# A two-block model on one core: order of the latent projections, packing of the output weights, place of the turned-weight copy, and 16-bit one-hot rows

## What is computed

```python
experts = jnp.take_along_axis(cand_i, pos, axis=-1).reshape(PEER_BLOCK, PEER_HEADS * PEER_TOPK)
gates = jax.nn.softmax(top_s, axis=-1).reshape(PEER_BLOCK, PEER_HEADS * PEER_TOPK)
hid = jax.nn.gelu(jnp.einsum('nkd,nd->nk', u, xb), approximate=False) * gates
return jnp.einsum('nk,nkd->nd', hid, v_table[experts])
```

```python
h = xn @ w_in
q_lat, kv_lat, k_rope, z = jnp.split(h, [384, 640, 704], axis=-1)
q = (rms_norm(q_lat, q_norm) @ w_q_up).reshape(B, S, 16, 192)
kv = (rms_norm(kv_lat, kv_norm) @ w_kv_up).reshape(B, S, 16, 256)
# rotary part of q and k, causal softmax over 16 heads of width 128 -> o
return (o.reshape(B, S, 2048) * jax.nn.silu(z)) @ w_out
```

## Time and profile before

| | us |
|---|---|
| median of 3 runs | 3790.28 |
| lowest and highest | 3776.75, 3790.76 |
| the profiled execution, its own time | 3789.53 |
| its span in the trace | 3787.7 |
| mean granted clock of TensorE | 0.961 |
| TensorE busy in the span | 3565.3 |

### The profile page before, as it was taken

How to read it: one execution, slowest core, us unless ns; L and a number is a source line. 1 busy time by engine, 2 the same in 40 slices (tenths; PEclk the granted TensorE clock), 3 DMA queues, 4 the chain that set the end, 5 groups by cost and what they waited for, 6 DMA issues and landing times.

```text
span 3787.7 us, 45651 instructions
## 1 busy us (share of the span) xinstructions
PE 3565.3 (94%) x16352; PEld 2906.0 (77%) x16352; DVE 1827.5 (48%) x3647; ACT 1178.8 (31%) x1578; POOL 915.3 (24%) x371
## 2 busy tenths in 40 slices
PE   7999799999999998999999899989999989988998
PEld 6776578878888887888888688878887756666886
DVE  1354526974444535454554656454442343314573
ACT  3232334333444441121121332233332334423322
POOL 2301234442333334444454200000000421121000
PEclk8987899999999999999999899999999999989999
DMA  2200123444446455544545222222222211112222
GB/s 95 73 17 34 39 83 117 145 139 161 160 160 205 158 177 200 211 177 192 207 177 197 92 99 95 94 83 96 98 94 97 78 63 38 40 45 84 94 89 89
DMA packets 141175, 434.90 MB, mean 115 GB/s; under 512 B 11152, under 2 KB 44176, under 8 KB 132496
## 3 DMA queue, kind: packets, MB, share of 16 engines
q1 hardware_dynamic: 141072, 433.50, 32.8%
HBM read 364.25 MB, written 69.21 MB: 114 GB/s over the span
## 4 chain that ended last, share of the span: by engine, by line
PE 86%; issue 6%; DVE 3%; ACT 1%; DMA 1%; POOL 1%; SPq 0%; POOLq 0%; DVEq 0%; ACTq 0%
PE ring_banks L235 22%; PE ring_banks L237 22%; PE ring_banks L236 22%; PE work_banks L1064 3%; PE work_banks L237 3%; PE work_banks L235 3%; PE work_banks L236 3%; POOL wlo L709 1%; PE ring_banks L1225 1%; PE ring_banks L945 1%; PE work_banks L1194 1%; PE work_banks L1197 1%; PE work_banks L908 1%; DMA slot<-u 1%; PE work_banks L758 0%
## 5 line engine op out<-in xcount | busy, mean ns | idle before, releaser
L235 PE MATMUL ring_banks<-xx,wlo 128*128 128x512 f32 x2960 | 1178.1, 398 | 57.2 <-DVE xx L1674 39.7
L237 PE MATMUL ring_banks<-xx,whi 128*128 128x512 f32 x2960 | 1164.9, 394 | 0.0
L709 POOL TENSOR_TENSOR wlo<-slot,whi 128x1024 fp32r<-128x1024 f32 x235 | 578.9, 2467 | 2103.5 <-ACT whi L1277 2103.5
L236 PE MATMUL ring_banks<-xx,whi 128*128 128x512 f32 x2512 | 988.6, 394 | 0.0
L1277 ACT ACTIVATE whi<-slot 128x1024 fp32r<-128x1024 f32 x427 | 451.3, 1060 | 1073.9 <-DMA slot<-w 653.6
L235 PEld LDWEIGHTS ring_banks<-xx,wlo 128*128 128x128 f32 x2960 | 565.3, 191 | 183.1 <-issue 56.4
L237 PEld LDWEIGHTS ring_banks<-xx,whi 128*128 128x128 f32 x2960 | 563.6, 190 | 119.3
L236 PEld LDWEIGHTS ring_banks<-xx,whi 128*128 128x128 f32 x2512 | 479.1, 191 | 96.7
L722 POOL TENSOR_TENSOR vlo<-v,vhi 128x1024 fp32r<-128x1024 f32 x128 | 325.0, 2569 | 379.7 <-ACT vhi L1509 379.7
L1986 DVE TENSOR_SCALAR oneI<-const,slot_row,slot_gate 128x128 f32<-128x128 f32 x512 | 191.8, 375 | 289.7 <-PE work_banks L1064 275.9
L1641 DVE TENSOR_TENSOR wlo<-slot,whi 128x1024 fp32r<-128x1024 f32 x192 | 239.1, 1247 | 164.7 <-ACT whi L1277 153.6
(11 more groups left out here) (342 smaller groups left out, 4334.6 us busy)
## 6 DMA issues: line engine op xcount, KB each, us to landing
slot<-w SPq DMA_DIRECT2D x301, 512.0 KB, 3.3
slot<-u SPq DMA_DIRECT2D x128, 512.0 KB, 3.8
v<-v SPq DMA_DIRECT2D x32, 2048.0 KB, 11.6
early<-early SPq DMA_DIRECT2D x128, 256.0 KB, 3.9
gates<-stage SPq DMA_DIRECT2D x16, 2048.0 KB, 13.8
gbuf<-gates SPq DMA_DIRECT2D x32, 1024.0 KB, 4.8
ge<-early SPq DMA_DIRECT2D x32, 1024.0 KB, 7.3
hT<-xT SPq DMA_DIRECT2D x1, 2048.0 KB, 7.5
```

Source lines behind the costliest of these rows:

```text
L235: pe.matmul(out, w[1], x[0], start=start, stop=False)
L236: pe.matmul(out, w[0], x[1], start=False, stop=False)
L237: return pe.matmul(out, w[0], x[0], start=False, stop=stop)
L709: pool.tensor_tensor(w_lo, slot[s % RING], w_hi.bitcast(F32), ALU.subtract).then_inc(split, 1)
```

## The change

1. The latents are projected before the gate. The squares and sums of q_lat come after latent tile 4, those of kv_lat after gate tile 0; roots and splits are interleaved with takes of tiles.
2. The output weights are packed in the order of their use, eight products to a slab (`OUT_ORDER`). Products of output tiles 0 and 1 begin in step 26; 14 products of tile 2 stand between the last step and the products that need the last pair. Slabs 4 to 6 are rounded inside the steps, and a semaphore m_q frees a slot.
3. In the third and fourth query block of a pair, and in the last pair, ScalarE copies the turned weights ahead of the next exponentials.
4. One-hot rows are made in bfloat16 for eight tokens at once, by comparing with rows that repeat one value 128 times; the gate is divided into three 16-bit parts, so a token has three products. VectorE, no longer GpSimd, makes the rests of the last 84 u slabs.
5. The output is sent in eight transfers, one for each channel tile.

```diff
 HIGH_AT_STEP = _high_at_step()
+def _out_order():
+    at_step = {26: [(0, k) for k in range(8)], 27: [(0, k) for k in range(8, 12)] + [(1, k) for k in range(4)],
+               28: [(1, k) for k in range(4, 8)], 29: [(1, k) for k in range(8, 12)],
+               30: [(0, 12), (0, 13)], 31: [(1, 12), (1, 13)]}
+    order, places = [], {}
+    for step, products in at_step.items():
+        places[step] = range(len(order), len(order) + len(products))
+        order += products
+    order += [(2, k) for k in range(14)] + [(r, k) for r in range(3) for k in (14, 15)]
+    return order + [(r, k) for r in range(3, 8) for k in range(16)], places
+OUT_ORDER, OUT_AT_STEP = _out_order()
+OUT_HIGH_AT_STEP = {28: 4, 29: 5, 31: 6}
...
-        oneI = region("oneI", 16, P)
-        oneJ = region("oneJ", 16, P)
+        region("ones_area", 16 * 2 * P)
+        oneI = halved("oneI", "ones_area", PARTS, 16, P)
+        oneJ = halved("oneJ", "ones_area", 16, P, at=16 * PARTS * P)
+        iota16 = halved("iota16", "ms", P)
+        places16 = halved("places16", "rt", 2, T)
+        gate1 = halved("gate1", "rstd", T)
+        gate2 = halved("gate2", "rstd", T, at=T)
+        rest2, rest1 = gt_, newt[:, 0:T]
+        hits = halved("hits", "sq", BATCH, P)
...
+                    for x in range(RING, n):
+                        last, k = OUT_ORDER[8 * (x - RING) + 7]
+                        if k == 15:
+                            sp.wait_ge(done, TILE_AT["mout"] + last + 1)
+                        else:
+                            sp.wait_ge(m_q, sum(OUT_ORDER[8 * y + 7][1] < 15 for y in range(x - RING + 1)))
+                        sp.dma_start(slot[(s0 + x) % RING], src[s0 + x - base].rearrange("p (k m) -> p k m", k=8)).then_inc(loaded[(s0 + x) % RING], 16)
                     return
...
-            sp.wait_ge(xnr, NORM_AT["fin2"] + KD)
-            sp.dma_start(a["out"], xn[:, :, 0:T]).then_inc(s_out, 16)
-            sp.wait_ge(s_out, 16)
+            for k in range(KD):
+                sp.wait_ge(xnr, NORM_AT["fin2"] + k + 1)
+                sp.dma_start(a["out"][:, k, :], xn[:, k, :]).then_inc(s_out, 16)
+            sp.wait_ge(s_out, 16 * KD)
...
+            split_slabs(U_AT, AHEAD * TT)
             with pool.Fori(0, 16) as i:
                 for b in range(2):
                     split_v(b, i)
-            split_slabs(SLAB_AT["mz"], SLAB_AT["pin1"] - SLAB_AT["mz"])
+            split_slabs(SLAB_AT["mlat"], SLAB_AT["pin1"] - SLAB_AT["mlat"])
...
-                                       oneJ[:, 4 * q + u, :], start=True, stop=True)
+                        for part in range(PARTS):
+                            mm = pe.matmul(psB[:, q, u * P:(u + 1) * P], oneI[:, part, 4 * q + u, :],
+                                           oneJ[:, 4 * q + u, :], start=part == 0, stop=part == PARTS - 1)
                     mm.then_inc(p_om, 1)
...
             norm("mla")
-            project8("mz", 16, fresh=(xnr, NORM_AT["mla"]))
-            for r in range(6):
+            project8("mlat", 4, fresh=(xnr, NORM_AT["mla"]))
+            for r in range(4, 6):
                 s, t = SLAB_AT["mlat"] + r, TILE_AT["mlat"] + r
                 slab_in(pe, s)
                 bank = free_bank(t)
                 for k in range(8):
                     mm = product(pe, bank, pick(slab(s), k), pick((xh, xlo), k, slice(0, T)), k == 0, k == 7)
                 mm.then_inc(done, 1)
-            norm("qlat")
-            norm("kvlat")
+                if r == 4:
+                    norm("qlat")
+            def norm_keys(r):
+                if r == 0:
+                    norm("kvlat")
+            project8("mz", 16, between=norm_keys)
...
-            def out_part(r, k0, k1):
-                for k in range(k0, k1):
-                    s = mout + 2 * r + k // 8
-                    if k % 8 == 0 or k == k0:
-                        slab_in(pe, s)
-                    if k % 2 == 0:
-                        pe.wait_ge(m_y, k // 2 + 1)
-                    mm = product(pe, psA[:, (tout + r) % RING, :], pick(slab(s), k % 8), pick((xx, mz_lo), k, slice(0, T)), k == 0, k == 15)
-                if k1 == 16:
+            def out_product(x):
+                r, k = OUT_ORDER[x]
+                if x % 8 == 0:
+                    slab_in(pe, mout + x // 8)
+                if k == 0:
+                    if r < 2:
+                        pe.wait_ge(out_, TILE_AT["mhead"] + len(HEAD_TILES))
+                    elif r < 4:
+                        pe.wait_ge(m_z, PAIRS)
+                    else:
+                        free_bank(tout + r)
+                if k % 2 == 0:
+                    pe.wait_ge(m_y, k // 2 + 1)
+                mm = product(pe, psA[:, (tout + r) % RING, :], pick(slab(mout + x // 8), x % 8), pick((xx, mz_lo), k, slice(0, T)),
+                             k == 0, k == 15)
+                if k == 15:
                     mm.then_inc(done, 1)
+                elif x % 8 == 7:
+                    mm.then_inc(m_q, 1)
             for j in range(4):
...
+                for x in OUT_AT_STEP.get(s, ()):
+                    out_product(x)
                 mla_weigh(s)
-            for r in range(2):
-                out_part(r, 14, 16)
-            for r in range(2, 8):
-                free_bank(tout + r)
-                out_part(r, 0, 16)
+            for x in range(OUT_AT_STEP[STEPS - 1].stop, len(OUT_ORDER)):
+                out_product(x)
...
+            for r in range(QL):
+                take_lat(r)
+            lat_squares("qlat", 0)
+            for r in range(QL, 6):
+                take_lat(r)
+            lat_root("qlat")
+            lat_squares("kvlat", QL)
+            lat_highs("qlat", 0)
+            take_mz(0)
+            take_mz(1)
+            lat_root("kvlat")
+            lat_highs("kvlat", QL)
+            take_mz(2)
+            take_mz(3)
...
             head0 = SLAB_AT["mhead"]
-            slab_high(head0)
...
                 n, tiles = s % TT, HEAD_TILES_AT[s]
-                if s + 1 < STEPS:
+                if n < 2 and tiles:
                     mla_exp(s + 1)
-                if n < 2 and tiles:
                     take_head(tiles[0])
-                act.wait_ge(m_t, s + 1)
-                if s:
-                    act.wait_ge(m_v, s)
-                act.activation(mpT[:, :, 0:n + 1, :], psB[:, 2:4, 0:(n + 1) * P].rearrange("p e (a b) -> p e a b", b=P),
-                               ACT.Copy).then_inc(m_c, 1)
+                    copy_turned(s)
+                else:
+                    copy_turned(s)
+                    if s + 1 < STEPS:
+                        mla_exp(s + 1)
                 if tiles:
                     take_head(tiles[-1])
                 if s in HIGH_AT_STEP:
                     slab_high(head0 + HIGH_AT_STEP[s])
+                if s in OUT_HIGH_AT_STEP:
+                    slab_high(SLAB_AT["mout"] + OUT_HIGH_AT_STEP[s])
...
-            def onehots(n0, i):
-                for q in range(4):
-                    if n0 + q >= 4:
-                        dve.wait_ge(p_om, at(n0 + q - 3, i, 4))
-                    for u in range(4):
-                        token = 4 * (n0 + q) + u
-                        c = slice(token, token + 1) if i is None else bass.ds(i * 16 + token, 1)
-                        b = 4 * q + u
-                        dve.tensor_scalar(oneI[:, b, :], iota, it_[:, c], gt_[:, c], ALU.is_equal, ALU.mult)
-                        ins = dve.tensor_scalar(oneJ[:, b, :], iota, jt_[:, c], None, ALU.is_equal)
-                    ins.then_inc(p_oh, 1)
+            step(dve.tensor_copy(iota16, iota))
             dve.wait_ge(p_tc, TT)
+            step(dve.tensor_copy(places16[:, 0, :], it_))
+            step(dve.tensor_copy(places16[:, 1, :], jt_))
+            step(dve.tensor_copy(gate1, gt_))
+            step.wait()
+            step(dve.tensor_tensor(rest1, gt_, gate1, ALU.subtract))
+            step.wait()
+            step(dve.tensor_copy(gate2, rest1))
+            step.wait()
+            step(dve.tensor_tensor(rest2, rest1, gate2, ALU.subtract))
+            step.wait()
+            def onehots(t0, i):
+                every = iota16.unsqueeze(1).to_broadcast([P, BATCH, P])
+                low = 0
+                for x in range(2 * STAGE // BATCH):
+                    token, b = t0 + BATCH * x, BATCH * (x % 2)
+                    c = slice(token, token + BATCH) if i is None else bass.ds(i * 2 * STAGE + token, BATCH)
+                    def row(v):
+                        return v[:, c].unsqueeze(2).to_broadcast([P, BATCH, P])
+                    if token >= 16:
+                        dve.wait_ge(p_om, at(token // 4 - 2, i, STAGE // 2))
+                    step(dve.tensor_tensor(oneJ[:, b:b + BATCH, :], every, row(places16[:, 1, :]), ALU.is_equal))
+                    step(dve.tensor_tensor(hits, every, row(places16[:, 0, :]), ALU.is_equal))
+                    step.wait()
```

(19 more changed lines are left out.)

86 lines of the change are left out of this document (54 added, 32 removed).

## The result

The changed kernel takes 3720.74 us (median of 4 runs, 3717.30 to 3723.22), 0.9826 of the kernel before, 95% interval 0.9805 to 0.9846. The forecast was 3729. In later runs beside other kernels it was 3720.16 us, ratio 0.9820 (0.9801 to 0.9840). The profiled execution has a span of 3720.0 us, 67.7 less than before.

What follows compares the result with a forecast made beforehand. TensorE, busy 94% of the span, was taken to bound the kernel. Terms of -10.8 (one-hots), -14 (latents), -33.2 (heads and output weights) and -2.5 (output transfers) took 3789.5 to 3729 us, range 3716 to 3742.

Steps and rivals of the forecast that it cites:

- the sum of -60.5: Whole kernel: one-hots -10.8, latents -14, heads and output weights -33.2, output transfers -2.5 us, from 3789.5 to 3729.
- The nearest row: One-hot stage, TensorE: two profiled 16-bit products 0.06 us apart, from which 0.061 a product was taken, -16 us.
- the rule that spoke against it: One-hot stage, TensorE: a skill page's 81 ns per load and product, making the stage 15 us longer instead of 16 shorter.
- instead of 0.25: One-hot stage, TensorE: 24 short products take 1.46 us against 1.71, saving 0.25 per eight tokens in 64 groups.
- as summed: One-hot stage: VectorE needs 7.2 us for eight tokens against TensorE's 8.3, so it stays hidden by 13%.
- the 1.5 us that the first instruction had lost before: Start of the one-hot stage: VectorE's first instruction loses 1.5 us again, within 4.9 us for six instructions.
- The step that carried this: One-hot stage, VectorE: GpSimd gives up its rests, so an instruction of 1024 elements takes 1.15 us, not 1.67.
- the 2.0 us for the rotary part: Around the latents: sines and turn start against gate takes and a head slab, leaving 2.0 us of TensorE's stretch.
- The sum of 25.7 from idle time: Heads and output: waits of 16.8, 5.4 and 5.6 us go, new ones of 0.6 and 1.5 come, -25.7.
- The clock term of 7.5: Heads: with most idle gaps gone, TensorE's work at the lower clock level speeds up, -7.5 us.
- The rival of waits that only move: Heads: late exponentials hold the next turn and scores, half of 27.8 us stays, 3743 us in all; chance 0.13.
- the range's 3.6: End of the kernel: eight output transfers gain 2.5 us, with a range of 0 to 3.6.

Runs made afterwards that it cites:

- the second profile: The changed kernel run and profiled once more with nothing altered: 3720.16 us, ratio 0.9820 to the kernel before.
- rests on GpSimd: Changed kernel with 16-bit one-hots kept, but the rests of all u slabs left on GpSimd: 3746.85 us, ratio 0.9899.
- the sines moved: Changed kernel with last slot transposes ahead of the last hidden tile, and sine and cosine ahead of the gate's last four takes: 3706.41 us, ratio 0.9781.
- gate first: Changed kernel with the latents projected behind the gate again, the rest kept: 3725.23 us, ratio 0.9840.
- both halves undone: Changed kernel with output weights packed by tile again and exponentials ahead of the copies again: 3757.33 us, ratio 0.9924.
- one output transfer: Changed kernel with the output sent again in one transfer of 2 MB: 3721.97 us, ratio 0.9836.
- exponentials first: Changed kernel with exponentials ahead of the copies of the turned weights everywhere, packing kept: 3734.26 us, ratio 0.9852.
- output by tile: Changed kernel with output weights packed by tile again, copies still ahead of the exponentials: 3737.58 us, ratio 0.9871.

## Why the prediction was right, point by point

| part | forecast | traces | alone, by experiment |
|---|---|---|---|
| one-hots | -10.8 | -12.7, or -13.4 without the 0.7 lost ahead of them | -13.4 (S -19.0, start +5.6) |
| latents first | -14 | -10.8 | -12.4, and -14.4 against the second profile |
| heads and output weights | -33.2 | -37.5 | -36.3 |
| eight transfers | -2.5 | -3.9 | -4.2 |
| not forecast: a norm's wait | 0 | -2.4 | none, differs by execution |

Every part but one brought more than forecast: the sum of -60.5 stands against a span 67.7 us shorter. The last row is luck of the one execution, and 2 us of it are given back in L.

**One-hots.** The nearest row (0.06 for a short product) was nearer than the rule that spoke against it: 0.055 in the trace, in groups of 24 between tiles. The page "TensorE: Matmul & The Clock Gate" of the Trainium skill, section "Back-to-back issue gap", has 81 ns for a sustained stream of loads and products; no run here has such a stream over more than 24 products, and in those of 24 the trace does not agree. The size was off: 0.38 us less for eight tokens instead of 0.25 would make -24, and S gave -19.0. The starts in both traces say where the five are. The stage has 48 groups of eight tokens and 32 of four, and the latter save only 0.155 us each (0.653 against 0.808): 1.2 us. TensorE's stall at 946 us was there before and grew from 4.3 to 6.3. There ScalarE waits for a slab, and SP had issued that slab behind two transfers of the gates; SP, then ScalarE, of the changed kernel:

```profile
927.61 10.89 SPq L693 DMA_DIRECT2D gates<-stage  x2
938.54 5.75 SPq L677 DMA_DIRECT2D slot<-u  x1
```
```profile
950.74 1.06 ACT L1326 ACTIVATE whi<-slot 128x1024 fp32r<-128x1024 f32 x1 [17.26 <-DMA slot<-u]
```

And the tiles between the groups took 2.9 us more in all (5.57 instead of 5.54 at the median), for a reason that stays open. VectorE's side in the stage came out as summed, 5.9 for the first group and 87% busy; its start did not, as said above: the 1.5 us that the first instruction had lost before did not come again, and the first product follows the last gate by 9.1 us, not by 10 to 11. The step that carried this, that GpSimd's leaving makes the price 1.15 and not 1.67, is what the run with rests on GpSimd shows: without that half, the part costs 12 us of S instead of gaining 19.

**Latents first.** The term that failed in size is the 2.0 us for the rotary part. I had named what stands ahead of the sines, a head slab and its transfer, but priced it as a shift of the chain; TensorE waits 4.35 us for ropek, with 3.4 to 6.8 us of half clock around it. The run with the sines moved took all of it back, 5.9 to 7.9 us. That the total is still near -14 (-13.2 for norm and latents together, and about -14.5 against gate first) is in part luck: the waits on squares and rests had brought half clock too, which I had not counted. From the norm to the heads TensorE was at the lower level for 34 us before, 38 with the gate first and 24 with the change.

**Heads and output.** The waits went as forecast, and the new ones are 2.2 us (forecast 2.1). The sum of 25.7 from idle time was low, since a gap costs more than its idle share: the copies alone gave 16.9 for 13.5 us of waits. The clock term of 7.5 is borne out: the estimates are 5.7 with the packing undone and 7.4 with both halves undone. It hangs mostly on the packing's gaps, where the prediction spoke of gaps of any kind. The rival of waits that only move is excluded: no wait on mp over 0.9.

**The end.** The last of eight transfers leaves 2.4 us, not 4.1. The gain of 3.9 to 4.2 lies beyond the range's 3.6: the part that does not shrink with the size was set too large.

What stays open: why profiled executions of kernels with the same code ahead of the one-hot stage differ there by up to 18 us. (The two profiles of the changed kernel agree within 0.2 us there, so it may hang on the kernel and not only on the execution.) The traces show where it lies. The first 500 us of the changed kernel, of one output transfer and of gate first:

```profile
0.00:500.00 500.00, 426.64 (x1885) 326.76 (x1886) 211.61 (x308) 154.42 (x263) 104.98 (x46) 0.86 0.15 52
```
```profile
0.00:500.00 500.00, 426.91 (x1932) 329.08 (x1933) 214.38 (x316) 159.25 (x270) 109.85 (x48) 0.88 0.15 52
```
```profile
0.00:500.00 500.00, 429.55 (x1959) 331.73 (x1960) 217.77 (x316) 162.50 (x274) 113.09 (x50) 0.89 0.16 55
```

TensorE was at the lower level for 144, 123 and 113 us of them, and the last transpose of the slots started at 843.5, 831.4 and 825.4. Half of the 31 us between the first and the last, and one wait without a releaser of 10.8 us instead of 14.0, are together about the 18. Why the level differs is open; no experiment was aimed at it. Whether the gates' transfers on another queue would remove the stall at 946 us wasn't tried.

## What to carry to other kernels

Moving elementwise work from GpSimd to a busy VectorE can be a gain where the instructions of the two hold each other up, as they did here: price VectorE's instructions by how many of them meet one of GpSimd, and each meeting at nearly the length of GpSimd's (here 66 meetings of 2.2 us). When a chain is hidden behind other work, look at the last short instruction that joins the two in an engine's list: two sines of 0.6 us behind a slab's transfer cost 6 to 8 us, though their input had been ready for 50. A forecast that comes true can hold terms that were wrong and cancelled; the first tile at 860.7 is one, the latents are another. Where executions differ by more than a part brings, compare stretches between the same two instructions, not totals.

## What the runs showed of the hardware

A VectorE instruction of 1.22 us took 3.39 when it started 0.5 us after a GpSimd instruction of 2.8 us, and 1.22 with GpSimd idle; 66 of 320 did so in that stage. Products of 16-bit numbers with 128 columns and weights of their own start 0.055 us apart in groups of 24. Over a wait of 1.66 us two starts lie 2.05 us apart instead of 0.23. The last of eight transfers of 256 KB is through 2.4 us after its issue, one of 2 MB 6.6 us after it. In the heads the granted clock stayed at its full level through waits of 1.66 us about every 27 us (exponentials first) and fell to half around waits of 2.2, 3.4 and 5.8 us (output by tile).
